# Mixture of experts on one Trainium2 core: gathering tokens by router group in front, and scattering once per group

## What is computed

```python
def moe(x, w_router, router_bias, w_gate, w_up, w_down):
    ...
    grouped = biased.reshape(b, s, N_GROUPS, EXPERTS_PER_GROUP)        # 4 groups of 4 experts
    group_score = jnp.sum(lax.top_k(grouped, TOP_K)[0], axis=-1)
    group_mask = jnp.argmax(group_score, axis=-1)[..., None] == jnp.arange(N_GROUPS)
    masked = jnp.where(group_mask[..., None], grouped, -jnp.inf).reshape(b, s, N_EXPERTS)
    _, expert_idx = lax.top_k(masked, TOP_K)                           # 2 experts, both of one group
    ...
    for e in range(N_EXPERTS):
        h = jax.nn.silu(jnp.einsum("bsd,df->bsf", x, w_gate[e])) * jnp.einsum("bsd,df->bsf", x, w_up[e])
        y = y + combine[..., e:e + 1] * jnp.einsum("bsf,fd->bsd", h, w_down[e])
    return y
```

## Time and profile before

| | |
|---|---|
| median of 3 runs | 1967.93 us (1955.69 to 1969.32) |
| the profiled execution | 1967.56 us, span 1965.8 us, granted TensorE clock 0.922 of full |
| PE busy | 1709.6 us (87%) |
| DVE busy | 1282.3 us (65%) |
| ACT busy | 854.1 us (43%) |
| DMA | 348.22 MB, mean 177 GB/s |
| experts' block, with the add after it | 1549.9 to 1944.6 us |

### The profile page before, as it was taken

How to read it: one execution, slowest core, us unless ns; L and a number is a source line. 1 busy time by engine, 2 the same in 40 slices (tenths; PEclk the granted TensorE clock), 3 DMA queues, 4 the chain that set the end, 5 groups by cost and what they waited for, 6 DMA issues and landing times. The chain is left out here.

```text
span 1965.8 us, 28190 instructions
## 1 busy us (share of the span) xinstructions
PE 1709.6 (87%) x11861; PEld 1571.9 (80%) x11861; DVE 1282.3 (65%) x1489; ACT 854.1 (43%) x1030; POOL 33.5 (2%) x48
## 2 busy tenths in 40 slices
PE   1899989999799998999699978778876599999994
PEld 1889878999699888999689967668766588888883
DVE  5777578788566376565459554355466578887875
ACT  2245434333345434343235612365142366666662
POOL 0100000000100000000000000000000000000000
PEclk8899999999899998999899989788689599999997
DMA  8965357899453245663555521123033378888771
GB/s 305 287 193 180 120 172 259 285 322 320 120 166 116 100 130 172 203 235 108 149 178 163 161 65 44 44 64 108 22 121 112 108 260 273 276 275 277 270 266 58
DMA packets 267011, 348.22 MB, mean 177 GB/s; under 512 B 14596, under 2 KB 222192, under 8 KB 266752
## 3 DMA queue, kind: packets, MB, share of 16 engines
q1 hardware_dynamic: 266880, 346.36, 53.4%
HBM read 345.29 MB, written 1.97 MB: 177 GB/s over the span
## 5 line engine op out<-in xcount | busy, mean ns | idle before, releaser
L457 PE MATMUL bank<-layer_split,hT_pair 128*128 128x256 f32 (+1 forms) x4224 | 517.1, 283 | 11.0 <-DVE hT_pair L314 4.8
L457 PEld LDWEIGHTS bank<-layer_split,hT_pair 128*128 128x128 f32 x4224 | 503.0, 192 | 17.0 <-issue 9.2
L184 DVE TENSOR_TENSOR layer_split<-layer_raw,layer_split 128x2048 fp32r<-128x2048 f32 x122 | 280.2, 2296 | 100.3 <-ACT layer_split L172 98.8
L172 ACT ACTIVATE layer_split<-layer_raw 128x2048 fp32r<-128x2048 f32 x122 | 233.7, 1915 | 200.9 <-PE bank L457 113.7
L184 DVE TENSOR_TENSOR expert_split<-expert_raw,expert_split 128x2048 fp32r<-128x2048 f32 x96 | 217.1, 2289 | 42.9 <-ACT expert_split L172 42.9
L457 PE MATMUL bank<-split_w,hT_pair 128*128 128x256 f32 (+1 forms) x1248 | 179.8, 308 | 31.5 <-PEq L599 13.7
L457 PEld LDWEIGHTS bank<-split_w,hT_pair 128*128 128x128 f32 x1248 | 170.2, 204 | 42.1 <-issue 34.7
L172 ACT ACTIVATE expert_split<-expert_raw 128x2048 fp32r<-128x2048 f32 x96 | 179.9, 1909 | 4.5 <-PEq L1715 4.5
L184 DVE TENSOR_TENSOR split_w<-raw_w,split_w 128x2048 fp32r<-128x2048 f32 x52 | 119.2, 2292 | 52.9 <-ACT split_w L172 52.4
L669 PE MATMUL bank<-layer_split,ffnh_aT 128*128 128x512 f32 x528 | 127.0, 396 | 2.8 <-DVE ffnh_aT L741 2.8
L172 ACT ACTIVATE split_w<-raw_w 128x2048 fp32r<-128x2048 f32 x52 | 99.4, 1912 | 61.7 <-PE bank L457 52.8
(11 more groups left out here) (447 smaller groups left out, 1996.5 us busy)
## 6 DMA issues: line engine op xcount, KB each, us to landing
layer_raw<-in_ada_w SPq DMA_DIRECT2D x48, 1024.0 KB, 6.1
layer_raw<-in_ffn_w_gate_up SPq DMA_DIRECT2D x44, 1024.0 KB, 5.2
raw_w<-in_w_in SPq DMA_DIRECT2D x40, 1024.0 KB, 5.1
layer_raw<-in_w_in SPq DMA_DIRECT2D x38, 1024.0 KB, 6.3
expert_raw<-in_w_gate SPq DMA_DIRECT2D x32, 1024.0 KB, 5.6
expert_raw<-in_w_up SPq DMA_DIRECT2D x32, 1024.0 KB, 5.2
expert_raw<-in_w_down SPq DMA_DIRECT2D x32, 1024.0 KB, 5.3
layer_raw<-in_ffn_w_down SPq DMA_DIRECT2D x22, 1024.0 KB, 5.0
```

The costliest lines, as they stand in the source:

```text
L172: self.nc.scalar.activation(self.pair[:, j % self.pairs, 0, 0:self.size[n]], self.raw[:, n % self.depth, 0:self.size[n]], ACT.Copy).then_i ...
L184: self.nc.vector.tensor_tensor(self.pair[:, j % self.pairs, 1, 0:self.size[n]], self.raw[:, n % self.depth, 0:self.size[n]], self.pair[:, ...
L457: ins = nc.tensor.matmul(out, lhs, rhs, start=c == 0 and tp + wp == 0, stop=c == job.k - 1 and tp == 1)
```

## The change

- Slots are counted per router group, not per expert: 128 slots for a group, whose four experts share its gathered rows. The fallback now depends on the largest group.
- All gathering stands in front: 16 steps (high and low part, 8 chunks) of 2 matmuls of 512 columns (four groups x 128 slots) through seven banks. Each is emptied by two copies of 256 columns on ACT or DVE. The four tables' turns stand between them, and four ring units are split there.
- Gate and up have a bank each: 24 matmuls of 512 columns instead of 48 of 256. ACT takes `Silu` of the gate, and DVE does one operation of 512 columns in place of four of 256.
- The hidden rows are turned and multiplied by the down weights one step later, after the next expert's gate and up. The down products of a group's four experts add up in banks 4 and 5.
- These banks are emptied, split and scattered once a group (4 x 2 matmuls of 512 columns), and DVE adds each piece to x from three spare banks. `scaled_add` goes away.
- Units are whole rows: gate and up 4 x 128 rows of 2 KB (before 8 x 128 pieces of 1 KB), down 2 x 128 rows of 4 KB (before 4 x 128 pieces of 2 KB). The down units of expert e-1 come after gate and up of e.

```diff
-            for e in range(N_EXPERTS):
-                for n in range(2):
-                    expert_units += [[(0, 8, 256, 0, 256, expert_half(name, e, n))] for name in ("w_gate_2", "w_up_2")]
-                for nb in range(2):
-                    expert_units.append([(0, 4, 512, 0, 512, A["w_down_2"][0, e, :, 512 * nb:512 * nb + 512]
+            for e in range(N_EXPERTS + 1):
+                if e < N_EXPERTS:
+                    for name in ("w_gate_2", "w_up_2"):
+                        expert_units += [[(0, 4, 512, 0, 512, rows_of(name, e, k0, 4))] for k0 in (0, 4)]
+                if e:
+                    expert_units += [[(0, 2, D, 0, D, rows_of("w_down_2", e - 1, k0, 2))] for k0 in (0, 2)]
...
-                scaled_add("moe", ALPHA)
...
+                    def hidden(e, u, bank):
+                        for i in range(2):
+                            ring.arrived(pe, u + i)
                             for c in range(4):
                                 for tp, wp in ((0, 0), (0, 1), (1, 0)):
+                                    ins = nc.tensor.matmul(ps[bank][:, :],
+                                                           gathered[e // PER // 2][:, tp, 4 * i + c, slot_cut(e // PER)],
+                                                           ring.view(u + i, wp, 4, 512)[:, c, :],
...
+                    for n in range(16):
...
+                        for t in range(TILES):
+                            ins = nc.tensor.matmul(ps[PICK[n % 7]][:, :], xP[:, part, t, c * P:(c + 1) * P],
+                                                   G[:, t, :, :].rearrange("p g s -> p (g s)"), start=t == 0, stop=t == 1)
...
+                    for e in range(N + 1):
+                        if e < N:
+                            if e:
+                                pe.wait_ge(gated, e)
+                            hidden(e, units_of(e)[0], GATE)
+                        if e:
+                            turn(e - 1)
+                        if e < N:
+                            if e:
+                                pe.wait_ge(acted, e)
+                            hidden(e, units_of(e)[0] + 2, UP)
+                        g = e // PER - 1
+                        if e % PER == 1 and g >= 0:
+                            scatter(g, (0, 1, 2))
+                        if e:
+                            down(e - 1)
+                        if e % PER == 1 and g >= 0:
+                            scatter(g, (3,))
+                    scatter(GROUPS - 1, (0, 1, 2, 3))
...
                 def _(act):
...
+                    for n in range(0, 16, 2):
+                        act.wait_ge(picked, n + 1)
+                        picked_out(n)
...
+                        if n in (4, 8, 12):
+                            ring.hi(act, n // 4)
+                    for e in range(N + 1):
+                        b = units_of(min(e, N - 1))[0] + (6 if e == N else 0)
+                        ring.hi(act, b + 4)
+                        if e < N:
+                            act.wait_ge(ring.used, b + 2)
...
+                            a.activation(silu[:, :], ps[GATE][:, :], ACT.Silu).then_inc(gated, 1)
+                        ring.hi(act, b + 5)
+                        if e:
+                            act.wait_ge(turned, e)
...
+                            a.activation(flat(aT[:, 0, :, :]), ps[TURN][:, :], ACT.Copy).then_inc(a_hi, 1)
+                        ring.hi(act, b + (8 if e else 6))
...
                 def _(dve):
...
+                    for e in range(N + 1):
+                        b = units_of(min(e, N - 1))[0] + (6 if e == N else 0)
+                        ring.lo(dve, b + 5)
+                        if e:
+                            dve.wait_ge(a_hi, e)
+                            v.tensor_tensor(flat(aT[:, 1, :, :]), ps[TURN][:, :], flat(aT[:, 0, :, :]).bitcast(FP),
+                                            ALU.subtract).then_inc(a_lo, 1)
+                        ring.lo(dve, b + 6)
+                        if e < N:
+                            dve.wait_ge(ring.used, b + 4)
+                            dve.wait_ge(gated, e + 1)
...
+                            v.scalar_tensor_tensor(act_[:, :], ps[UP][:, :], w_slot[:, e:e + 1], silu[:, :],
+                                                   ALU.mult, ALU.mult).then_inc(acted, 1)
+                        g = e // PER - 1
+                        if e % PER == 1 and g >= 0:
+                            add(g, (0, 1, 2))
+                        ring.lo(dve, b + (8 if e else 6))
```

More of the change, by code:

```diff
@@ L1745, in sparse_experts @@
[L1745 to L1749, removed]
+                    for t in range(TILES):
+                        for g in range(GROUPS):
+                            ins = v.tensor_scalar(G[:, t, g, :], const("slot"), key[:, t, g:g + 1], None, ALU.is_equal)
@@ L1757, in _ @@
                 def _(pe):
[L1758 to L1767, removed]
-                        for part in range(2):
-                            for t in range(TILES):
-                                ins = nc.tensor.matmul(ps[3][:, part * S:(part + 1) * S], xP[:, part, t, c * P:(c + 1) * P],
-                                                       G[:, pair % 2, t, :], start=t == 0, stop=t == 1)
-                        ins.then_inc(picked, 1)
@@ L1786, in scatter @@
-                    def scatter(e):
-                        pe.wait_ge(o_lo, 2 * e + 2)
-                        for t in range(TILES):
-                            for nb in range(2):
-                                for part in range(2):
-                                    ins = nc.tensor.matmul(ps[4 + 2 * t + nb][:, :], GT[:, e % 2, t * P:(t + 1) * P],
-                                                           oP[:, part, nb * 512:(nb + 1) * 512],
-                                                           start=e == 0 and part == 0, stop=e == N - 1 and part == 1)
-                        ins.then_inc(scattered, 1)
@@ new lines, in scatter @@
+                    def scatter(g, pieces):
+                        for j in pieces:
+                            t, nb = j // 2, j % 2
+                            if j == 0:
+                                pe.wait_ge(o_lo, 2 * g + 2)
+                            if 4 * g + j >= 3:
+                                pe.wait_ge(added, 4 * g + j - 2)
+                            for part in range(2):
+                                ins = nc.tensor.matmul(ps[SPARE[(4 * g + j) % 3]][:, :], GT[:, g, t * P:(t + 1) * P],
+                                                       oP[:, part, nb * 512:(nb + 1) * 512], start=part == 0, stop=part == 1)
+                            ins.then_inc(scattered, 1)
@@ new lines, in _, with picked_out @@
+                    scatter(GROUPS - 1, (0, 1, 2, 3))
+                def picked_out(n):
+                    part, c = n // 8, n % 8
+                    src = ps[PICK[n % 7]][:, :].rearrange("p (i s) -> p i s", i=2)
+                    for i in range(2):
+                        dst = gathered[i][:, part, c, :]
+                        if n % 2 == 0:
+                            ins = a.activation(dst, src[:, i, :], ACT.Copy)
+                        else:
+                            ins = v.tensor_copy(dst, src[:, i, :])
+                    ins.then_inc(picked_dve if n % 2 else picked_act, 1)
@@ new lines, in add @@
+                    def add(g, pieces):
+                        for j in pieces:
+                            t, cut = j // 2, slice((j % 2) * 512, (j % 2) * 512 + 512)
+                            dve.wait_ge(scattered, 4 * g + j + 1)
+                            bank = ps[SPARE[(4 * g + j) % 3]][:, :]
+                            if g == 0:
+                                ins = v.scalar_tensor_tensor(x[:, t, cut], x[:, t, cut], ALPHA, bank, ALU.mult, ALU.add)
+                            else:
+                                ins = v.tensor_tensor(x[:, t, cut], x[:, t, cut], bank, ALU.add)
+                            ins.then_inc(added, 1)
```

272 lines of the change are left out of this document (125 added, 147 removed).

## The result

| | before | after |
|---|---|---|
| median of the runs beside each other | 1965.55 us (4 runs) | 1880.52 us (1877.80 to 1881.11, 4 runs) |
| ratio after / before | | 0.9572, 95% interval 0.9544 to 0.9600 |
| the profiled execution, span | 1967.56, 1965.8 us | 1880.32, 1878.5 us |
| first pick to last add | 1550.85 to 1944.63: 393.8 us | 1548.53 to 1857.37: 308.8 us |

The forecast was 1887 us, the range 1870 to 1908. The spans differ by 87.3 us: 84.9 in the experts' block (first pick to last add), 2.8 because the stretch ahead of it ended sooner, less 0.5 us by which the small block between them, with the tables, grew.

What follows compares the result with a forecast made beforehand. PE was taken to set the period. Front 20.1, expert 0 13.0, loop 261.0, scatters 5.6 and end 14.3 gave 314.0 us against 394.7, so 1967.56 - 80.7 = 1886.9, forecast 1887 us, range 1870 to 1908.

Steps and rivals of the forecast that it cites:

- Front: Gathering ahead of the first gate: first product at 1570.0 us, 3.3 us later than before; 20.1 us counted from 1549.9.
- Expert 0: First expert's gate and up: 2 x 5.6 us plus 1.8 for the cold clock, 13.0 us against 25.8.
- Loop: PE's work per expert: three products of 5.6 us and transposes of 0.6, 17.4 us in place of 23.16, 15 times.
- Scatters: Group scatters inside the loop: three at 1.87 us, 5.6 us in all.
- End: From the end of expert 15's up to the last add: 14.3 us, including 1.0 for the hidden product.
- the chain of 5.9 us: ACT and DVE work from gate to turned rows, beside 6.2 us of PE work: slack 0.3 us, no wait counted.
- the only wait of PE that recurs: Old loop's wait for the turned rows' low part: 0.54 us per expert, 8.7 over 14; so less PE work shortens the period.
- The DMA step: Weight loads: 361 GB/s needed; full engines give 339 with 1 KB pieces, 404 with longer ones, so DMA keeps up.
- DMA becomes the bound: Rival on weight loads: full engines give 339 to 350 GB/s at any piece size, 9 to 18 us more, about 1900; chance 0.17.
- Late rows: Rival at the down product: PE waits 1.6 us per expert for the turned rows, 24 us more, 1911; chance 0.16.
- The dense path: Rival: a group with more than 128 tokens triggers the fallback of 32 blocks, +584 us, 2471; chance 0.02.
- little: Rival in the loop: handovers keep it at 22 us per expert, total about 1955; chance 0.03.

Runs made afterwards that it cites:

- a_silu3: Changed kernel with the gate's Silu taken three times on ACT, two into a spare tile; block 317.2 us (+8.3), total 1888.9 us, ratio 0.9627.
- a_half_pieces: Changed kernel with each weight unit loaded as two column halves, pieces of 1 KB and 2 KB; block 308.4 us (-0.4), total 1884.9 us.
- a_serial: Changed kernel with the down product back right after its own expert's up product; block 354.0 us (+45.2), total 1923.3 us, ratio 0.9794.
- b_neither: Kernel before without the picks of pairs 1 to 7 and without 12 of 16 scatters; block 393.8 us (0.0), total 1962.7 us, ratio 0.9999.
- b_no_picks: Kernel before without the picks of pairs 1 to 7 and their emptyings; block 375.6 us (-18.2), total 1946.2 us, ratio 0.9923.
- b_no_scatter: Kernel before with 12 of 16 scatters left out; block 405.2 us (+11.4), total 1973.5 us, ratio 1.0054.

## Why the prediction was right, and where its reasons were not

**The sum held, term by term.** Front: forecast 18.6 us from first pick to first gate, measured 18.5. Expert 0: 13.0 forecast, 13.2 measured (18.8 less a gate of 5.6), cold start included, although PE stood idle for 4.1 us before it and not for 8. Loop: 17.4 an expert forecast, 17.22 measured, since four transposes block PE for 0.35 us and not for the 0.6 that their busy time had suggested: 2.7 us over 15. Scatters: 1.83 us each (periods of 19.04 with one) against 1.87. End: 14.3 forecast, 13.8 measured, and its nearness is partly luck. The 1.0 us for the hidden product was not paid, since the fifteenth step already holds the down product that covers it; the rest of the end took 0.5 us more than drawn. That makes the block 3.7 us shorter than forecast, and the earlier end of the stretch ahead of it, 2.8 us that I could not know, makes up the rest of the 6.5 between 1887 and 1880.5. The table load of Silu came once at expert 0; a second, of 1.28 us, came at the last layer norm, which I had not foreseen, but ACT was waiting there for DVE's result:

```profile
1861.23 1.28 ACT L1618 ACT_TABLE_LOAD   x1 [8.40 <-issue]
...
1865.11 1.06 ACT L1618 ACTIVATE ln_junk<-x 128x1024 f32<-128x1024 f32 x1 [2.59 <-DVE x L1606]
```

**The order was right.** The sum of the new period was built from what PE still does, with the chain drawn out against it. The slack that I put at 0.3 us was 0.34, by `a_silu3`, and the chain of 5.9 us took 5.5 (1708.02 to 1713.54). That I costed the new order, and not only removed work from the old one, is what made the sum come out.

**The reading of the old kernel fell short.** "It is the only wait of PE that recurs, so taking PE work out shortens the period until the next limit is met" is true, but it suggests that PE's own work was all that stood in the way, save 0.54 us. The next limit, the chain from the hidden products to the down product, stood 1.3 us behind (21.96 against 23.25): the scatter and part of the picks were lying in its gaps. By the same reading I expected 53 us from leaving both out of the old order; the block gave 0.0. A wait that other work fills does not show in the waits. The forecast did not suffer, because it never subtracted that work from the old period.

**The DMA step was wrong, with no harm.** I divided 325 GB/s by the busy share 0.96 of the earlier trace rows and called 339 the ceiling of 1 KB pieces, and 404 that of longer ones. But the same pieces gave 358 at a share of 1.04 when the loop asked for them. A share of 1.00 is no ceiling, and two of the windows of the earlier trace rows said so, with 1.02 and 1.04. So the rival "DMA becomes the bound" was priced on a ceiling that is not there, and the longer pieces bought no time here. The loop's mean of 357 is what PE asked for, scatters included. Over three periods without a scatter the changed kernel drew 368 GB/s, and `a_half_pieces` in the same window 370:

```profile
1600.43:1652.08 51.65, 51.65 (x230) 41.83 (x230) 44.96 (x26) 38.41 (x27) 0.00 (x0) 1.00 1.01 368
```
```profile
1600.43:1652.08 51.65, 51.65 (x230) 41.88 (x229) 44.62 (x25) 37.58 (x25) 0.00 (x0) 1.00 1.05 370
```

PE was busy throughout in both, so no run shows a limit. The Trainium skill, "DMA: Bandwidth & Descriptors", section "Bandwidth", puts the limit for loads from HBM at about 358 GB/s. These windows lie above it, as do the 408 over 20 us.

**The other rivals.** Late rows did not come, though 1 us of delay on ACT was enough to bring them. The dense path did not run. The gain was no "little" one: no wait of PE recurred in the loop.

## What to carry to other kernels

Before counting removed work as gain, draw the chain through one period without it: what fills a gap hides that gap, so it has no row in the waits, and the busy share (97% here) does not tell filler from need. Where the profile has a stretch without that work, as the last two experts here, read the period there: it shows the next limit. Moving the dependent product one step later took the waits out of this loop, and in that order PE work counts in full; in the old order, taking out picks gave 18 of 31 us, taking out scatters a loss. The two halves were worth about the same, 45 us for the later product (`a_serial`) and 40 for all the rest, of which only the width and the length of the pieces were taken singly. Compare such changes by the length of the stretch that they touch, when what lies ahead moves by more than the effect.

## What was not expected of the hardware

Short gaps of PE, in a loop where it was otherwise dense, brought the granted clock down to 1.2 GHz for the start of the next product. In `b_neither` PE stood idle for 1.97 us, ran four transposes (0.66 us) and stood idle for 1.41 us. In all 13 experts with both gaps the down product behind them took 7.2 to 7.4 us instead of 5.86, and the mean clock from 1600 to 1900 us was 0.94. With gaps of 0.84 and 1.41 us (`a_serial`) it happened at four of 13 experts. With 1.41 us alone it never happened (15 experts of `b_no_picks`, clock 1.00); that kernel's one slow down product, 7.17 us at its first expert, had both gaps ahead of it. The pair of gaps does not bring it every time: at the last expert of `b_no_scatter`, 1.97 and 1.41 us were followed by 5.87. Less work on PE thus made the kernel slower in `b_no_scatter`.

Also, 24 matmuls of 512 columns and 48 of 256 differ by less than 0.1 us here (2.1 us over 32 such runs), although the second form has 24 more weight loads.
